# Layer three's statistics: once per chunk on VectorE and four matmuls instead of sixteen, with a third gate buffer

## The reference, cut to what matters

```python
a, ag, z = jnp.split(jnp.einsum('bsd,de->bse', h, w_in_c), 3, axis=-1)   # D=1024 -> 3 x E=2048
glu = a * jax.nn.sigmoid(ag)
ext, conv_c_new = with_history(glu, hist_c, CCONV_W - 1)                 # 30 rows of history
y = causal_depthwise_conv(ext, w_conv_c) + b_conv_c                      # 31 taps
y = jax.nn.silu(layer_norm(y, ln_c_g, ln_c_b))                           # mean, variance over E
out = jnp.einsum('bse,ed->bsd', y * jax.nn.silu(z), w_out_c)
```

## Time and profile before

| | |
|---|---|
| Median of 3 runs | 2303.03 us (2300.75 to 2444.65) |
| The profiled execution: its own time | 2300.88 us |
| Its span on the slowest core (core 1) | 2299.1 us |
| Spans of the 8 cores | 2289.2 to 2299.1 us |
| TensorE busy | 2120.9 us, 92% of the span |
| VectorE busy | 1301.6 us, 57% |
| ScalarE busy | 721.7 us, 31% |
| Layer three's gate and convolution stage | about 1205 to 1591 us of the span |
| z stage of layer three | about 1575 to 1745 us |

### The profile page before, as it was taken

How to read it: one execution, slowest core, us unless ns; L and a number is a source line. 1 busy time by engine, 2 the same in 40 slices (tenths; PEclk the granted TensorE clock), 3 DMA queues, 4 the chain that set the end, 5 groups by cost and what they waited for, 6 DMA issues and landing times.

```text
span 2299.1 us, 38646 instructions; the slowest of 8 cores (2289.2 to 2299.1 us)
## 1 busy us (share of the span) xinstructions
PE 2120.9 (92%) x12651; PEld 1169.1 (51%) x12651; DVE 1301.6 (57%) x2565; ACT 721.7 (31%) x1243; POOL 198.8 (9%) x373
## 2 busy tenths in 40 slices
PE   1898999999899999999998999997888989999997
PEld 0344555555455555555544555554444545555553
DVE  2478663234576666665445545454665467776545
ACT  3553233334311111111432322232544433323121
POOL 2002001200101111100010000000000010000000
PEclk7999999999999999999999999999999999999999
DMA  9512726625633333334566666643566562023434
GB/s 187 122 41 38 120 34 128 105 68 160 113 47 56 56 56 56 56 46 84 158 147 109 103 101 94 100 87 77 140 149 159 161 113 39 11 38 47 93 103 141
DMA packets 145235, 215.04 MB, mean 94 GB/s; under 512 B 16816, under 2 KB 85552, under 8 KB 144304
## 3 DMA queue, kind: packets, MB, share of 16 engines
q0 software_dynamic: 50544, 96.00, 29.0%
q1 hardware_dynamic: 94496, 116.56, 17.8%
HBM read 255.07 MB, written 53.43 MB: 134 GB/s over the span
## 4 chain that ended last, share of the span: by engine, by line
PE 75%; DVE 9%; DMA 8%; issue 4%; ACT 3%; DVEq 0%; ACTq 0%; SPq 0%; POOL 0%; POOLq 0%
PE ps L468 50%; PE ps L612 17%; DMA big<-xt 3%; PE ps L1026 3%; DMA big<-ybuf 2%; DVE big L528 2%; PE ps L522 2%; PE ps L797 2%; DMA gbuf<-big 1%; DVE big L804 1%; DMA ybuf<-big 1%; PE ps L1040 1%; DVE big L1122 1%; DVE big L532 1%; DVE big L1125 1%
## 5 line engine op out<-in xcount | busy, mean ns | idle before, releaser
L468 PE MATMUL ps<-big 128*128 128x384 bf16 (+4 forms) x7360 | 1361.8, 344 | 63.0 <-ACT big L1151 31.9
L468 PEld LDWEIGHTS ps<-big 128*128 128x128 bf16 x7360 | 714.9, 98 | 651.2 <-issue 88.2
L612 PE MATMUL ps<-big 128*128 128x384 bf16 (+4 forms) x2560 | 485.4, 344 | 3.2 <-ACT big L1151 3.1
L612 PEld LDWEIGHTS ps<-big 128*128 128x128 bf16 x2560 | 251.1, 98 | 210.0 <-issue 9.2
L636 DVE SCALAR_TENSOR_TENSOR big<-ps,big 128x384 f32<-128x384 f32 (+3 forms) x192 | 111.2, 582 | 220.9 <-PE ps L612 214.7
L521 ACT ACTIVATE big<-big 128x384 bf16<-128x384 f32 (+4 forms) x200 | 107.0, 553 | 317.0 <-DVE big L636 272.7
L797 PE MATMUL ps<-big 128*128 128x512 bf16 (+1 forms) x576 | 131.6, 389 | 20.4 <-DMA big<-w_v 19.4
L1066 DVE TENSOR_TENSOR big<-big,ps 128x384 bf16<-128x384 f32 (+1 forms) x96 | 50.3, 524 | 168.2 <-ACT big L1062 157.0
L964 ACT ACTIVATE big<-ps 128x384 bf16<-128x384 f32 (+3 forms) x80 | 42.0, 525 | 282.3 <-PE ps L468 282.3
L522 PE MATMUL ps<-big 128*128 128x384 bf16 (+4 forms) x200 | 68.9, 359 | 58.5 <-ACT big L521 57.8
L528 DVE RECIPROCAL big<-big 128x384 f32<-128x384 f32 (+4 forms) x25 | 70.3, 2812 | 92.6 <-ACT big L527 92.6
(11 more groups left out here) (115 smaller groups left out, 1627.8 us busy)
## 6 DMA issues: line engine op xcount, KB each, us to landing
big<-w_ada POOLq DMA_DIRECT2D x96, 256.0 KB, 7.0
big<-w_in_b POOLq DMA_DIRECT2D x64, 256.0 KB, 6.2
big<-w_in_c POOLq DMA_DIRECT2D x48, 256.0 KB, 5.5
big<-xbuf SPq DMA_DIRECT2D x56, 192.0 KB, 5.5
xbuf<-big SPq DMA_DIRECT2D x48, 192.0 KB, 3.7
gbuf<-big SPq DMA_DIRECT2D x16, 548.0 KB, 9.9
big<-gbuf SPq DMA_DIRECT2D x16, 548.0 KB, 4.7
ybuf<-big SPq DMA_DIRECT2D x16, 540.0 KB, 3.5
```

What stands on the lines that cost most here:

```text
L468: ins = h.matmul(out, lhsT=lhs(k), rhs=rhs(k), start=(k == 0), stop=(k == n - 1))
L612: ins = h.matmul(bank(b)[:, 0:w], lhsT=w8[e // 8][:, e % 8, :], rhs=YS[:, e, x0:x0 + w], start=(i == 0), stop=(i == 15))
```

## The change

- The squares and sums are no longer made per group. When all eight groups of a chunk's row are written, VectorE does six instructions on the whole row (2,160 columns, bf16): the square of the row; the two halves of the square added; two sums of quarters of the row itself; the second halving of the square; and the sum of the two quarter sums. What is left is 540 columns of sums and 540 of squares.
- TensorE then does four matmuls of 270 columns per chunk instead of sixteen.
- The VectorE work is delayed by three items (`defer(3, sums)`), and the four matmuls by six more after that.
- The gate buffers are three (`GB[c % 3]`). The third lies where layer two's input tiles were, and is cleared by a VectorE memset placed after chunk 1's last tile. The DRAM buffers stay two.
- The mean and deviation buffers (`LM`) and the scratch for squares and sums are placed elsewhere.

```diff
-        GB = [tmp("gb%d" % i, 1024 + i * 1096, 8 * CPH, True) for i in range(2)]
+        GB = [tmp("gb%d" % i, 1024 + i * 1096, 8 * CPH, True) for i in range(2)] + [xsb("gb2", 6856, 8 * CPH, True)]
...
-        SQC = [Buf("sqc%d" % i, NRM_o + i * 135, YPH, True) for i in range(6)]
-        LM = [Buf("lm%d" % i, NRM_o + 810 + i * YPH, YPH) for i in range(2)]
+        SQR = Buf("sqr", NRM_o, 8 * YPH, True)
+        PYA = Buf("pya", NRM_o + 1080, 2 * YPH, True)
+        PYB = tmp("pyb", 4312, 2 * YPH, True)
+        LM = [xsb("lm%d" % i, 2160 + i * YPH, YPH) for i in range(2)]
...
-                q = SQC[nsc[0] % 6]
-                nsc[0] += 1
-                s.op("dve", lambda h, y=y, q=q: h.tensor_tensor(out=q.v, in0=y, in1=y, op=ALU.mult), reads=["yp.%d.%d" % (c, g)], writes=[q.key])
-
-                def st(c=c, g=g, y=y, q=q):
+
+            def sums(c=c):
+                R = YS[:, c, 0:8 * YPH]
+                yk = ["yp.%d.%d" % (c, g) for g in range(8)]
+                h1, h2, h3 = 2 * YPH, 4 * YPH, 6 * YPH
+                s.op("dve", lambda h: h.tensor_tensor(out=SQR.v, in0=R, in1=R, op=ALU.mult), reads=yk, writes=[SQR.key])
+                s.op("dve", lambda h: h.tensor_tensor(out=SQR.v[:, 0:h2], in0=SQR.v[:, 0:h2], in1=SQR.v[:, h2:], op=ALU.add), reads=[SQR.key], writes=[SQR.key])
+                s.op("dve", lambda h: h.tensor_tensor(out=PYA.v, in0=R[:, 0:h1], in1=R[:, h1:h2], op=ALU.add), reads=yk, writes=[PYA.key])
+                s.op("dve", lambda h: h.tensor_tensor(out=PYB.v, in0=R[:, h2:h3], in1=R[:, h3:], op=ALU.add), reads=yk, writes=[PYB.key])
+                s.op("dve", lambda h: h.tensor_tensor(out=SQR.v[:, 0:h1], in0=SQR.v[:, 0:h1], in1=SQR.v[:, h1:h2], op=ALU.add), reads=[SQR.key], writes=[SQR.key])
+                s.op("dve", lambda h: h.tensor_tensor(out=PYA.v, in0=PYA.v, in1=PYB.v, op=ALU.add), reads=[PYA.key, PYB.key], writes=[PYA.key])
+
+                def st():
                     def f2(h):
-                        h.matmul(bank(6)[:, 0:YPH], lhsT=bones, rhs=y, start=(c == 0 and g == 0), stop=(c == 15 and g == 7))
-                        return h.matmul(bank(7)[:, 0:YPH], lhsT=bones, rhs=q.v, start=(c == 0 and g == 0), stop=(c == 15 and g == 7))
-                    s.op("pe", f2, reads=["cst", "yp.%d.%d" % (c, g), q.key], writes=bk(6, 7))
-                defer(3, st)
+                        ins = None
+                        for k in range(2):
+                            h.matmul(bank(6)[:, 0:YPH], lhsT=bones, rhs=PYA.v[:, k * YPH:(k + 1) * YPH], start=(c == 0 and k == 0), stop=(c == 15 and k == 1))
+                            ins = h.matmul(bank(7)[:, 0:YPH], lhsT=bones, rhs=SQR.v[:, k * YPH:(k + 1) * YPH], start=(c == 0 and k == 0), stop=(c == 15 and k == 1))
+                        return ins
+                    s.op("pe", f2, reads=["cst", PYA.key, SQR.key], writes=bk(6, 7))
+                defer(6, st)
+            defer(3, sums)
...
-            G = GB[c % 2]
+            G = GB[c % 3]
...
+        s.op("dve", lambda h: h.memset(GB[2].v, 0.0), writes=[GB[2].key])
         build_more(5)
```

More of the change, by code:

```diff
@@ L1011, in build_more @@
                     build(*build_q.pop(0))
-        nsc = [0]
         def conv(c):
@@ L1080, in away @@
                 done(("in", 2, 16 * j + c))
-            s.dma("sp", "gw%d" % (c % 2), gbuf[c % 2].rearrange("a p m -> p a m"), v3(GB[c % 2].v, 8), reads=[GB[c % 2].key], writes=["gd%d" % (c % 2)])
+            s.dma("sp", "gw%d" % (c % 2), gbuf[c % 2].rearrange("a p m -> p a m"), v3(GB[c % 3].v, 8), reads=[GB[c % 3].key], writes=["gd%d" % (c % 2)])
         def back(c):
```

## The result

The changed kernel takes 2268.81 us in the median of 4 runs (2266.16 to 2269.29), against 2300.75 (2297.64 to 2303.03) for the kernel before on the same chip. In some executions the cores of one die take some per cent longer at a lower granted clock, whichever kernel runs, and the times and ratios compared here are of executions without that. The ratio is 0.986, with a 95% interval of 0.9841 to 0.9879: 1.4% faster. The interval is clear of no change, but the gain is less than the 2% that counts as told from it here. The time is 1.8 us above the forecast of 2267. The profiled execution took 2269.09 us (span 2267.3), and its slowest core is core 1, as before. All rows of after are from that core unless another is named.

What follows compares the result with a forecast made beforehand. TensorE was taken as the convolution stage's bound, by its own time and gaps. -33.9 - 3.4 - 4.5 + 1.5 + 2.7 + 2 = -35.6 us from 2300.88 gives 2265, plus 2.1 for the median: 2267 us, range 2257 to 2280.

Steps and rivals of the forecast that it cites:

- Part 1: Steady chunks: twelve fewer statistics matmuls (1.38 us) and no gaps (1.71 us) make a chunk 19.86 us; -33.9 us over 11.
- Part 2: VectorE's six whole-row instructions take 3.8 to 4.0 us per chunk, covered with 1.8 us to spare; nothing on the path.
- Part 3: Start: third buffer ends chunk 2's write wait, conv(0) at 1259.0, -3.4 us; conv(0) to conv(3) -4.5, despite chunk 3's 3.0 wait.
- Part 4: End: conv(15) waits longer for data, lower clock level there +1.5 us, uncovered row work before the norm +2.7 us.
- Part 5: Steady chunks' write and read through DRAM, with 16.66 us left, just hidden or just late: +2 us, bounds 0 and 7.
- The trip sets the pace: Rival, chance 0.20: DRAM trips 2 us late in 11 chunks, 22 us instead of 2; 2287 us, or 2277 at half.
- the row's work is slow: Rival, chance 0.05: VectorE's whole-row work takes 6.5 us, costing 16 us more over chunks, chunk 3 and end; 2283 us.
- Everything hides: Rival, chance 0.10: DRAM trips never late, chunk 3 doesn't wait, conv(15)'s data come 2 us sooner; 45 us gained, 2258 us.
- Slower than before: Rival, chance 0.03: a 16.4 us write in every chunk makes each trip 22.1 us; +22 us, 2325 us.

Runs made afterwards that it cites:

- gate_first: The changed kernel with the projection of the gate's sigmoid half put before the other half's in every tile; ratio 0.9849, chunks 19.86 to 19.87 us.
- sixteen_late: The changed kernel without halving sums: one whole-row square, sixteen statistics matmuls in one piece where the four stood; median 2281.50 us, ratio 0.9917.
- square_4x: The changed kernel with the whole-row square done four times, same result; 2303.79 us in one execution, chunks 22.25 us.
- square_twice: The changed kernel with the whole-row square done twice, same result; 2277.63 us, chunks 20.33 to 20.34 us.
- gate_and_group: The changed kernel with gate_first's projection order and, for chunk 15 alone, a square and two statistics matmuls per group as before the change; ratio 0.9825.
- z_early2: The changed kernel with two z-stage tiles projected before conv(15) and chunk 15's read placed behind conv(14); median 2276.33 us, ratio 0.9889.

## Why the prediction was right, and where its steps were not

The total came out 1.8 us from the forecast. A part of that is luck. The sum was 3.8 us too good for core 1: +4.9 for the chunks, -2.0 for the trips, -1.3 from conv(0) to conv(3), +1.4 for the end, +0.8 for the rest, so errors of both signs met in it. And the 2.1 us put on top of the sum came from the median of three executions of which one took 2444.65 us.

**Part 1 failed in one step**: "The convolution no longer waits for squares, so the 1.71 us of gaps go too; what comes next there is ScalarE's bias". What came next was the wait for a PSUM bank that VectorE's gate holds, 0.47 us in a chunk and 5 us in eleven. The trace of before doesn't name it, since TensorE stood at the same moment for the first squares (L1036), and only the later reason is shown:

```profile
1409.77 0.48 DVE L1073 TENSOR_TENSOR big<-big,ps 128x32 f32<-128x32 f32 x2 [0.17 <-DVE big L1066]
...
1410.62 0.28 PE L1040 MATMUL ps<-big 128*128 128x270 bf16 x1 [0.52 <-DVE big L1036]
```

It could have been worked out. These history writes end 2.63 us after the convolution's start at 1407.62, and the prediction itself has this 2.6 in part 2; the fifth group, which needs their bank, is due after 20 x 0.115 = 2.30 us. gate_first removed exactly this wait and gave the 19.86 us. So of the 1.71 us of gaps 1.22 went. The 1.38 us for the matmuls are shown by sixteen_late.

**Part 2 held.** The three durations forecast as 1.32, 0.73 and 0.44 us are 1.279, 0.723 and 0.433, and the six instructions take 3.5 us from the first start to the last end (3.7 in the chunk shown above), for 3.8 to 4.0 forecast. The slack of 1.8 us measured 2.25 in square_4x. There is no pause in between: the sums of 540 columns, 0.43 us long, start 0.35 us apart. The Trainium skill, "VectorE: DVE Perf Modes" (The DRAIN you can't avoid), says that the next instruction starts only when the pipe is empty, after about the duration less 266 ns, and points to an exception for one that is not held; in this kernel every one of the six is like the exception.

**Part 3** has the right mechanism at chunk 2, and its 1259.0 was met with luck. In this execution the chunk began 0.71 us later and TensorE went on another 0.14 later, while the matmuls behind the stop took 9.24 us instead of the 10.1 counted; the granted clock there was 0.81, and the sum had kept a row of before at 0.65. From the start of chunk 2 the gain is 4.1 us on core 1 and 2.9 in the mean over the cores, for 3.4 forecast. In chunk 3 the wait for the row was 1.49 us where 3.0 were forecast: the five builds took 7.1 us where 5 x 1.48 = 7.4 were counted, the row's work 3.5 where 4.0 were, and TensorE came 0.5 us later, held by part 1's bank wait. That wait took 1.0 us in conv(0) and conv(1), and the microsecond for late data and clock was not needed on core 1: -5.8 instead of -4.5. It is the term with the least certainty: in square_twice, with 1.38 us more of VectorE, conv(1) to conv(3) took 3 to 7 us longer, for 1.4 forecast.

**Part 4** had each mechanism and sized two of them too small. conv(15) did wait for its data (3.14 us), did run at the lower level on core 1, and the row's work did stand bare before the norm, 3.4 us more where 2.7 were forecast. The lower level cost 2.8 us and not 1.5. The prediction shows no step that leads from its eight matmuls of the earlier trace rows to the 1.5; the granted clock over them was 0.65, between the levels, and at 0.50 core 1's first twenty matmuls alone lost 2.2 us. It did not strike every core: five of the eight kept 1.00, and so the mean way from conv(15) to the norm grew by 4.2 us, which happens to be the forecast sum of the two terms.

**Part 5** counted +2 for trips and none was late in a steady chunk. The chunk above shows it: chunk 9's write left at 1411.26 and had landed by 1421.40, and the read's 3.9 us end at 1425.3, 3.1 us before conv(9). With chunks of 20.34 us a trip has 17.1 us (1411.26 to 1428.40) and not 16.66; the longest of the eleven took 15.7 on core 1, and 16.9 on core 0, with 0.2 to spare. At the forecast length of a chunk some trips are late: in gate_first one convolution of the steady stretch waited for `gbuf` on each of three cores, 0.22, 0.44 and 0.47 us. So "just hidden or just late" was right, and +2 was too much even there. The medians of the stage (KB, us to landing; reads, then writes):

```profile
big<-gbuf SPq DMA_DIRECT2D x14, 548.0 KB, 4.1
gbuf<-big SPq DMA_DIRECT2D x13, 548.0 KB, 9.7
```

The upper bound of 17.3 us put together the longest of either leg in the earlier trace rows, which don't fall on the same chunk. The Trainium skill, "DMA: Bandwidth & Descriptors" (Anatomy of one DMA), would give about 3.3 us for either leg as an estimate, from a fit for DMAs that GpSimd issues, where these are SyncE's; the reads are near it, and the writes to DRAM take three times as long. So its consequence, no late trip in a steady chunk, came true for the wrong reason, and its other one, that conv(15) doesn't wait, is false.

Of the rivals, none happened as a whole. "The trip sets the pace" would have shown waits for `gbuf` in most chunks, and there is one; "the row's work is slow" is refuted by the durations. "Everything hides" was right that no steady trip is late, but chunk 3 did wait and a chunk took 20.34 us. "Slower than before" took its 16.4 us from a write that it saw among loads "in the same queues". From 1237 to 1254 us the loads' queue had 63.7% of the DMA engines' time and the queue of this write 20.3%, so the two shared the engines and not the queue; whether this slowed the write is not shown.

## What to carry to other kernels

When a wait is removed, look for the second holder of the same instruction: which buffer or PSUM bank does it need, and which engine's last access frees it. The trace of before names only the one that came last, and here two projections in the other order, at no cost, gave back what the change had left lying. And when work is taken off a loop's path into the shadow of the next iteration, the last iteration has no shadow: write that one the old way. That was worth 3.1 us on the way from conv(15) to the norm here; how much of it reaches the end was not measured by itself.

## What the runs showed of the hardware

The clock after a stop. TensorE's granted clock in the last convolution was 1.00 after stops of 1.82 us (core 2), 2.40 us (core 0) and 3.01 us (core 6), and 0.50 after 3.14 us (core 1), all in the one execution; with it matmuls of 270 columns start 0.115 or 0.225 us apart. On cores 3 and 4 of that execution it was 0.69 over the first 5.4 us after stops of only 2.12 and 2.38 us, and the way to the norm took 12.5 us instead of 10.9. In gate_and_group stops of 3.54 us on core 1 and 4.57 us on core 4 went before first pieces of 2.47 and 4.66 us. So a stop of 2 to 3.5 us costs only itself on one core and up to 2.8 us more on another, and its length alone doesn't tell which. What decides it stays open. With the stop filled (z_early2) all eight cores kept the full clock there. Equal kernels end some microseconds apart for this alone.

Two transfers of the same size through DRAM can differ twofold: in this stage on core 1 the 548 KB from SBUF took 6.5 to 14.7 us to land (median 9.7), the same 548 KB back 3.6 to 8.6 (median 4.1). The two differ in direction, but also in layout and in what runs beside them, and which of these makes the difference is not shown.

VectorE's bf16 products scale by columns nearly as forecast up to 2160 columns: 294 ns for 270, 425 for 512 and 1279 for 2160, which is 0.54 ns a column at first and 0.52 from there on.
